# A 1024-column modulation weight tile over four column tiles of the TensorE array, 256 columns each, instead of two of 512

## The reference, cut to what matters

```python
mod = silu(cond) @ w_mod[l] + b_mod[l]          # cond = c, c_ctx; w_mod[l] is (1024, 6144)
shift1, scale1, gate1, shift2, scale2, gate2 = split(mod, 6)
h = rms_norm(x, g1) * (1 + scale1) + shift1     # then q/k/v projection
x = x + gate1 * (attention(h) @ w_out[l])       # heads A (window), B (differential), C (grouped query)
h2 = rms_norm(x, g2) * (1 + scale2) + shift2
x = x + gate2 * peer(h2)                        # 8 heads, top 16 of 128*128 one-neuron experts each
```

## Time and profile before

| what | value |
| --- | --- |
| runs (us) | 4694.56, 4710.6, 4721.75 |
| median (us) | 4710.6 |
| span of the profiled execution (us) | 4711.4 |
| time of the profiled execution apart from the span | not given |
| TensorE busy | 3609.5 us, 77% |
| VectorE busy | 2815.4 us, 60% |
| mean granted TensorE clock | 0.953 |
| attention stage of layer 0 (first scores to end of its transposes) | 255 to 501 us |
| attention stage of layer 1 | 2570 to 2815 us |

### The profile page before, as it was taken

The page is one execution under the profiler, slowest core; times in us unless marked ns, Lnnn a source line. Parts: engine busy times, 40 slices in busy tenths (PEclk is TensorE's granted clock), DMA queues, the critical chain, the costliest instruction groups (busy, mean ns, idle before and its releaser), DMA issues.

```text
span 4711.4 us, 42538 instructions
## 1 busy us (share of the span) xinstructions
PE 3609.5 (77%) x14116; PEld 1664.6 (35%) x14116; DVE 2815.4 (60%) x6114; ACT 1462.1 (31%) x4289; POOL 1394.7 (30%) x1475
## 2 busy tenths in 40 slices
PE   5988796777777777777779888877777777777776
PEld 2554462323222222232236455422222222222222
DVE  3645676746746757654456456776576575675544
ACT  2245422222222222222232553222222222222222
POOL 1022003333433333433310120033333333343332
PEclk7998998999999999999999888999999999999998
DMA  4242128999999999999922302299999999999996
GB/s 179 64 146 90 36 72 332 383 405 414 412 415 419 412 416 415 414 404 420 419 107 67 129 15 67 93 407 411 409 416 407 418 417 416 404 414 415 419 415 283
DMA packets 213532, 1460.21 MB, mean 310 GB/s; under 512 B 23936, under 2 KB 24192, under 8 KB 48448
## 3 DMA queue, kind: packets, MB, share of 16 engines
q0 software_dynamic: 185952, 1355.11, 70.2%
q1 hardware_dynamic: 27360, 102.39, 6.6%
HBM read 1453.21 MB, written 4.19 MB: 309 GB/s over the span
## 4 chain that ended last, share of the span: by engine, by line
DMA 40%; PE 35%; DVE 13%; ACT 7%; issue 4%; POOL 0%; SPq 0%; DVEq 0%; ACTq 0%; POOLq 0%
DMA work<-expert_dram,work 22%; PE psum L787 18%; DMA hT<-expert_dram,work 17%; PE psum L563 7%; DVE work L1466 3%; DVE hT L1466 2%; ACT work L1008 2%; PE psum L635 2%; PE psum L574 2%; PE psum L663 1%; ACT work L998 1%; PE psum L684 1%; DVE work L1127 1%; PE psum L598 1%; DVE stat L1226 1%
## 5 line engine op out<-in xcount | busy, mean ns | idle before, releaser
L787 PE MATMUL psum<-work 128*128 128x512 f32 x3416 | 1611.7, 616 | 564.8 <-ACT work L1008 564.8
L1466 DVE SCALAR_TENSOR_TENSOR work<-work,psum 128x1024 f32<-128x1024 f32 x854 | 1041.7, 1220 | 855.1 <-DMA work<-expert_dram,work 854.6
L1521 POOL DMA_INDIRECT work<-expert_dram,work x854 | 832.3, 975 | 1472.2 <-PE psum L787 1324.8
L787 PEld LDWEIGHTS psum<-work 128*128 128x128 f32 x3416 | 629.0, 193 | 1536.9 <-ACT work L1008 897.6
L787 PE MATMUL psum<-hT,work 128*128 128x512 f32 x1704 | 809.4, 619 | 293.8 <-ACT work L1008 293.8
L998 ACT ACTIVATE work<-work,xinv 128x2 f32<-128x2 f32 x640 | 189.1, 295 | 2352.5 <-DVE work L1466 1574.7
L1466 DVE SCALAR_TENSOR_TENSOR hT<-hT,psum 128x1024 f32<-128x1024 f32 x426 | 519.7, 1220 | 422.5 <-DMA hT<-expert_dram,work 422.1
L1521 POOL DMA_INDIRECT hT<-expert_dram,work x426 | 416.4, 978 | 806.1 <-PE psum L787 659.8
L787 PEld LDWEIGHTS psum<-hT,work 128*128 128x128 f32 x1704 | 314.3, 194 | 782.3 <-ACT work L1008 462.1
L563 PE MATMUL psum<-hT,split 128*128 128x128 f16 (+1 forms) x2880 | 424.6, 307 | 60.3 <-DVE hT L1158 60.3
L1008 ACT ACTIVATE work<-const,work 128x128 f32<-128x128 f32 x1280 | 434.1, 386 | 0.0
(11 more groups left out here) (177 smaller groups left out, 2751.9 us busy)
## 6 DMA issues: line engine op xcount, KB each, us to landing
ring<-w_mod_dram SPq DMA_DIRECT2D x96, 512.0 KB, 3.9
ring<-w_in_dram SPq DMA_DIRECT2D x40, 512.0 KB, 3.6
ring<-w_query_dram SPq DMA_DIRECT2D x32, 512.0 KB, 3.6
work<-expert_dram,work POOLq DMA_INDIRECT x854, 8.5
ring<-w_out_dram SPq DMA_DIRECT2D x16, 512.0 KB, 3.6
hT<-expert_dram,work POOLq DMA_INDIRECT x426, 8.5
work<-rpb_dram POOLq DMA_DIRECT2D x2, 2688.0 KB, 14.3
xT<-xT_dram SPq DMA_DIRECT2D x1, 2560.0 KB, 11.9
```

The costliest lines, as they stand in the source:

```text
L787: last = pe.matmul(out[:, cols_], diag[:, n % NDIAG, :], rows[n % NBUF][:, D + 512 * half:D + 512 * half + 512], start=(s == 0), stop=(s = ...
L1466: dve.scalar_tensor_tensor(u, u, 1.0, pair[t % 2], ALU.mult, ALU.mult, accum_out=act_in[:, s:s + 1]).then_inc(dot_done, 1)
L1521: pool.indirect_dma_start(rows[n % NBUF], None, a[f"expert{l}"], bass.IndirectOffsetOnAxis(expert[:, t % 2, s:s + 1], 0)).then_inc(row_in[ ...
```

## The change

The weight tile goes through four column tiles of 256 columns (`MQ` = 4, `MW` = 256): results lie in rows 0, 32, 64 and 96 (two each), in the first 256 columns of the bank. ScalarE copies four 2x256 results instead of two 2x512. The transposes of a chunk are still eight, now two for each of four row groups, and they go into four banks (24 columns each, for all six chunks) instead of two (48 columns each). VectorE's bias addition makes four instructions of half the size instead of two. The loads, the ring and the place of every slot stay.

```diff
+MQ = 4
+MW = KC * P // MQ
...
-        modps = [[psum[:, bank + x, lo:lo + NMOD].rearrange("p (c i s) -> p c i s", i=4, s=2) for x in range(2)]
+        modps = [[psum[:, bank + x, lo:lo + 2 * NMOD // MQ].rearrange("p (c i s) -> p c i s", i=MW // P, s=2)
+                  for x in range(MQ)]
                  for bank, lo in ((4, 0), (0, 0), (0, NMOD))]
...
-            return work[32 * x:32 * x + 2, at_:at_ + 512]
+            return work[32 * x:32 * x + 2, at_:at_ + MW]
...
-                for x in range(2):
-                    last = pe.matmul(psum[32 * x:32 * x + 2, mod_home(l, c)[0], :], cT[:, k, :],
-                                     ringx[:, n % RING, 512 * x:512 * x + 512], start=(k == 0), stop=(k == KC - 1))
+                for x in range(MQ):
+                    last = pe.matmul(psum[32 * x:32 * x + 2, mod_home(l, c)[0], 0:MW], cT[:, k, :],
+                                     ringx[:, n % RING, MW * x:MW * x + MW], start=(k == 0), stop=(k == KC - 1))
...
-                for x in range(2):
+                for x in range(MQ):
                     unit = const[32 * x:32 * x + 2, CO["ident"] + 32 * x:CO["ident"] + 32 * x + 2]
-                    for i in range(4):
+                    for i in range(MW // P):
...
-                for x in range(2):
-                    last = act.activation(mrow(l, c, x), psum[32 * x:32 * x + 2, mod_home(l, c)[0], :], ACT.Copy)
+                for x in range(MQ):
+                    last = act.activation(mrow(l, c, x), psum[32 * x:32 * x + 2, mod_home(l, c)[0], 0:MW], ACT.Copy)
...
-                out = modT[:, l, lo:hi_, :].rearrange("p (c x i) s -> p c x i s", x=2, i=4)
-                b = b.rearrange("p (c x i) -> p c x i", x=2, i=4)
-                for x in range(2):
+                out = modT[:, l, lo:hi_, :].rearrange("p (c x i) s -> p c x i s", x=MQ, i=MW // P)
+                b = b.rearrange("p (c x i) -> p c x i", x=MQ, i=MW // P)
+                for x in range(MQ):
                     last = dve.tensor_tensor(out[:, :, x], mod_home(l, lo // 8)[2][x][:, lo // 8:hi_ // 8],
-                                             b[:, :, x].unsqueeze(3).to_broadcast([P, (hi_ - lo) // 8, 4, 2]), ALU.add)
+                                             b[:, :, x].unsqueeze(3).to_broadcast([P, (hi_ - lo) // 8, MW // P, 2]), ALU.add)
```

## The result

| | before | after |
| --- | --- | --- |
| median of 20 runs (us) | 4716.58 (4694.56 to 4732.68) | 4683.65 (4671.0 to 4710.14) |
| ratio, 95% interval | 1 | 0.9936 [0.9923, 0.9949] |
| span of the profiled execution (us) | 4711.4 | 4679.0 |
| mean granted clock | 0.953 | 0.952 |
| layer 0: first scores; from there to the scores of pair 49 | 255.17; 236.95 | 251.49; 221.33 |

The kernel became faster by 0.64%, some 30 us (24 to 36 by the interval). Of the 32.4 us between the two profiled spans 3.7 lie ahead of layer 0's first scores, 15.6 in its attention and 11.3 in layer 1's; between the two stages 0.6 went the other way, and 2.5 lie behind pair 49 of layer 1, where the change touches nothing but the last transposes and bias additions.

A forecast was written before the change was run, and what follows sets the result against it. TensorE was taken to bound the attention's A pairs; 16.3 + 5.1 + 2.8 + 1.5 - 0.5 = 25.2 us off 4711.4 gives 4686.2, or 4685.4 against the median, rounded up to 4686; range 4674 to 4708.

The forecast's parts named there:

- A slot: Two weight tiles in an attention pair, 40 slots in all: 0.86 us for 1.72 with four column tiles side by side.
- A pairs: Attention pairs bound by TensorE, 22 slots: 0.74 us saved in each, 16.3 us, the rest lost waiting for copies L916.
- B pairs: Attention pairs with 18 slots: eight slots save 0.64 us each, the others nothing, 5.1 us.
- half clock: Slots at half clock: excess busy time of 5.7 us, of which half goes, 2.8 us saved.
- The two kinds of slots: In B pairs: slots in pairs with value products save 0.64 us, those in pairs without save nothing.
- The start: The 16 tiles ahead of layer 0: loads issued up to 2.6 us earlier, 1.5 us taken as saved.
- ScalarE's copies: Four copies for two in each of twelve chunks: 0.15 us more for each of ten attention chunks, -0.5 us overall.
- The stages together: Attention stages: layer 0 some 14 us shorter and layer 1 some 10.
- No more than two at once: Rival in the slots: four tiles run two at a time, nothing gained, 4711 us; chance 0.10.
- the order rule: Part of the no-gain rival: each matmul's two records must pass one behind the other; 0.04 of its 0.10 chance.
- The partial case: Rival: next bounds close in sooner or tiles lose overlap, a slot gives 0.3 us, 12 us, 4699 us; chance 0.10.
- The clock, the rival on the slower side: Shorter slots let the clock fall in B pairs with slots, +28 us, 4722 us; chance 0.10.

The follow-up runs named there:

- e4: Kernel after, but only the first of the four column tiles computed, its result copied in place of all four; ratio to before 0.9945, slot 0.96 us.
- e3: Kernel after, but its 256-column matmuls go to two column tiles instead of four; ratio to before 1.0009, slot 1.83 us.
- e2: Kernel after, but two column tiles at the start and four only in the attention stages; ratio to before 0.9947.
- e1: Kernel after, but four column tiles only at the start and two in the attention stages; ratio to before 1.0008.
- e6: Kernel after, but ScalarE copies a chunk's four results by one instruction over partitions 0 to 97; ratio to before 0.9937.
- e9: Kernel after, plus one unread 512-column matmul in each of pairs 22 to 31 of layer 1; ratio to before 0.9932.
- e10: Kernel after, plus one unread 256-column matmul in each of pairs 22 to 31 of layer 1; ratio to before 0.9928.
- e5: Kernel after, but all four matmuls of a weight tile go to one column tile; ratio to before 1.0131, slot 3.56 us.
- e7: Kernel after, but seven of eight attention weight tiles multiplied over only 8 columns of each 256; ratio to before 0.9911.

## Why the prediction was right

It said 4686 us (-0.52%), between 4674 and 4708, and it became 4683.65 (-0.64%). Term by term, with means over the profiles that share the code where there are several:

- **A slot.** Four steps of 0.215 us, 0.86 us saved, the next scores 0.95 us behind the slot's start: measured four steps, 1.82 - 0.98 = 0.84 us saved. e4 shows that the four run without loss.
- **A pairs, 16.3 us.** The A cycle was to be 18.6 us and is 18.68, both at full clock. The late copies L916 (now L919) are late as named. Pairs 0 to 14 take 59.40 us for 69.47 in layer 0 and 59.08 for 65.93 in layer 1, 16.9 us together. That 10.1 and 6.9 us are so unlike is the clock of the kernel before: 0.90 in these pairs of layer 0 and 0.95 in those of layer 1. In e3, whose slots are as long as before, it is the other way round, 66.08 us at 0.95 and 69.52 at 0.90. The means over the profiles give 8.9 and 7.9 us, 16.8 together. The prediction had no clock in this term, and that it comes out so near is in part luck.
- **B pairs 5.1 and half clock 2.8 us.** By the means, what lies behind pair 14 in the stages gives 4.9 and 2.6 us, 7.5 for 7.9. The two kinds of slots are as told: pairs 19 to 21 of layer 0, with one slot of each kind and the full clock in both kernels, take 13.28 us for 13.89, 0.61 less where 0.64 was forecast. The half-clock term is read as the prediction read it, from L577 alone in the slots' stretches:

```profile
257.00:390.15 133.15, 27.22 (x384) 7.83 (x384) 0.88 0.54 190
2559.00:2640.00 81.00, 17.93 (x256) 4.93 (x256) 0.93 0.57 197
```

  Warm slots would be busy 40 x 1.04 = 41.6 us and are 45.15, an excess of 3.5 us where it was 5.7: 2.1 us saved for 2.8 in this pair of profiles (e2's excess is 4.2).
- **The start, 1.5 us.** The pair of profiles has 3.7 us. The mean over ten profiles has 1.8, of which 0.95 is the earlier issue of xT, the mechanism named. What more the profile after has stands in the projection of q, k and v, where the trace has one spell at half clock (1.2 GHz) in place of two. The other profiles with four column tiles at the start don't have the first scores so early, e1 apart, so I put it down to scatter.
- **ScalarE's copies, -0.5 us: the mis-sized term.** "0.38 us, started before the last has drained, and four of them take between 1.1 and 1.5 us", so 0.15 us more for a chunk. One is 0.372 us as said, but four take 1.52 us, and a chunk costs 0.35 us more. In the kernel after each of them starts 0.01 us after the one ahead has ended (records of 0.357 to 0.377 us, 0.386 us apart), while of the two copies L919 of 128 rows the second starts 0.11 to 0.13 us before the first has ended. The two L834 of the earlier trace rows don't overlap either: 0.570 and 0.588 us in 1.17. The overlap belongs to the one kind of copy and was carried over to the other. It cost nothing all the same, since e6, which takes away all of it and 0.8 us more, is no faster.
- **The stages together.** Some 14 and 10 us were expected. The mean over profiles has 236.35 - 222.58 = 13.8 us in layer 0 (before, e1, e3 against after, e2, e9, e10) and 234.8 - 224.2 = 10.6 us in layer 1 (against after, e2).

With the start this makes 26.1 us; the terms of the sum made 25.2. The medians stand 32.9 us apart and the interval is 24 to 36 us, so the sum lies inside it, near its lower end. What the ratio has beyond the sum, some 4 us, has no cause that a run shows, and needs none: it lies within the interval, and the code outside the stages, next to unchanged, scatters by 10 us and more from profile to profile.

**The rivals.** No more than two at once fell with the slot and with e4. For the order rule, of which the prediction spoke: if the two records of one matmul had to pass ahead of the next column tile's first, the four first records couldn't start within 0.02 us, and a slot of eight matmuls would have nine steps (before, with four matmuls, five). They do start so, and a slot has four steps. In e5 the records on one column tile start at least 0.215 us apart, so the four that start together belong to the four column tiles. The Trainium skill says that matmuls stay in program order ("TensorE: Matmul & The Clock Gate", section "Step-by-step: what each phase is for"). Read of single records this does not hold here, and the measurement decides; read of whole matmuls nothing in the trace speaks against it: of a weight tile's eight records the last to start is the one that signals its end. The partial case fell: 0.84 us in the slot and 24.4 / 40 = 0.61 us in the stages, not 0.3. The Trainium skill's figure of 2.38 for three column tiles ("TensorE: Matmul & The Clock Gate", section "Measured speedup vs the span model") would by the prediction's estimate have given 1.09 us for the steps of a slot. They take 0.86; with one column tile the 16 steps of e5 take 3.47 us, 4.0 times that, and to the next scores it is 3.56 / 0.98 = 3.6 times. The 19 us that the estimate made of it are below the interval. The clock, the rival on the slower side, moved the right way and not far: 0.85 for 0.89 in the B pairs with slots of layer 0, 0.01 lower over the stages in the first pair of profiles and some 0.02 in the means. e7 shows it go on, to 0.69 in pairs 15 to 31 of layer 0, as still more work is taken away.

## What to carry to other kernels

A matmul with few output rows leaves most of the array's columns idle. Its moving columns can be spread over four column tiles, and the time of a stream of such matmuls then falls nearly by the number of tiles; making it narrower without other column tiles gives nothing. What reaches the end is read from the waits behind it, slot by slot: here 0.84 us a slot became some 0.6, since ScalarE's copies and exponentials were close behind. When the rest of the work is then taken out and the stage hardly gets shorter, that doesn't yet say that the work was hidden: here 10 us came back in one part of the stages and 6 were lost in the rest, 4 of them where the clock fell. Look at the parts before believing the sum. To show a gain of a few us a median isn't enough: give the length of the stage in several profiles, since one scatters by 4 us.

## What the runs showed of the hardware that was not expected

- Four float32 records on four column tiles start within 0.020 us of one another, each 0.007 us behind the last, and the next four come 0.215 us after the first. With one, two or four column tiles the step of 256 columns is 0.215 to 0.217 us.
- The fixed part behind a slot: 0.98 - 4 x 0.215 = 0.12 us from the end of its steps to the next scores' weight load, for 0.10 before.
- ScalarE's copy out of PSUM goes by columns and hardly by rows: 2x256 takes 0.372 us, 98x256 0.394 us. Four of the first in a row take 1.52 us, without overlap, while two copies of 128x512 one behind the other (0.60 us each) overlap by 0.11 to 0.13 us.
- Work taken from a stretch with much waiting can lower the granted clock there: 0.85 to 0.69 in pairs 15 to 31 of layer 0 when the slots were made thin. In the A pairs ahead of them it didn't (0.91 and then 0.94).
